# Two attentions of a two-block transformer kernel: a low part in eight pieces, a table loaded ahead, fewer fillers, key tiles one by one

## What is computed

```python
for i in range(DEPTH):                       # two layers
    hn = rms_norm(h, norm_pre[i])
    ...
    # layer 0: 12 heads, 64 + 32 rotary features; layer 1: 12 heads of 64, forget gates added to the logits
    main = mla_mixer(...) if i % 2 == 0 else fox_mixer(...)
    mem_out = memory_attention(q_m, k_m, v_m)      # 4 heads over 256 memory tokens
    y = jnp.concatenate([main, mem_out], axis=-1) * jax.nn.silu(gate)
    h = h + rms_norm(y @ w_out[i], norm_post[i])

def causal_block_attention(q, k, v, scale, log_f_cum=None):
    ...
    s = jnp.where(mask, s, -jnp.inf)
    p = jax.nn.softmax(s, axis=-1)
    return jnp.einsum('bhqk,bkhd->bqhd', p, v)
```

## Time and profile before

| | us |
|---|---|
| median of three runs | 1983.44 |
| lowest, highest | 1981.88, 1983.7 |
| the profiled execution's own time | 1981.69 |
| its span | 1980.0 |
| TensorE (PE) busy | 1931.6 (98%) |
| VectorE (DVE) busy | 1100.9 (56%) |
| GpSimd (POOL) busy | 786.6 (40%) |
| ScalarE (ACT) busy | 767.0 (39%) |

### The profile page before, as it was taken

One profiled execution on the slowest core, in us unless ns is written; L12 is line 12 of the kernel. 1 busy time (PEld: TensorE's weight loads), 2 busy tenths in 40 slices (PEclk: granted clock), 3 DMA queues, 4 the chain that ended last, 5 costly groups with the idle time before them and its releaser, 6 DMA issues.

```text
span 1980.0 us, 23818 instructions
## 1 busy us (share of the span) xinstructions
PE 1931.6 (98%) x9905; PEld 1538.7 (78%) x9905; DVE 1100.9 (56%) x1514; ACT 767.0 (39%) x1175; POOL 786.6 (40%) x345
## 2 busy tenths in 40 slices
PE   7999999999999999999999999999999999999998
PEld 6877566988657699977788888787977878888886
DVE  5333767557776659544678747865811355512533
ACT  5335554421463431265323223324376333222331
POOL 2233643433563452122343444343532434444432
PEclk9999999999999999999999999999999999999999
DMA  8224004365303351121254444453430222233221
GB/s 257 72 48 124 31 1 139 120 196 176 107 1 101 113 170 65 43 85 59 71 164 143 144 143 143 132 159 106 143 113 22 83 78 95 85 100 113 77 80 57
DMA packets 212059, 205.95 MB, mean 104 GB/s; under 512 B 21351, under 2 KB 209003, under 8 KB 211952
## 3 DMA queue, kind: packets, MB, share of 16 engines
q1 hardware_dynamic: 209369, 200.36, 31.6%
q0 software_dynamic: 1472, 3.72, 0.7%
q10 hardware_dynamic: 1111, 0.36, 0.1%
HBM read 201.44 MB, written 2.11 MB: 103 GB/s over the span
## 4 chain that ended last, share of the span: by engine, by line
PE 86%; ACT 4%; DVE 4%; POOL 2%; issue 1%; DMA 1%; ACTq 0%; SPq 0%; DVEq 0%
PE bank L543 55%; PE bank L1128 16%; PE bank L784 2%; PE bank L484 2%; POOL wl L2352 2%; PE bank L951 1%; PE bank L833 1%; PE bank L808 1%; DMA ring<-in_w_mem_kv 1%; PE bank L1186 1%; ACT probs L1488 1%; PE bank L1196 1%; ACT wh L1339 1%; PE bank L533 1%; PE bank L566 1%
## 5 line engine op out<-in xcount | busy, mean ns | idle before, releaser
L2352 POOL TENSOR_TENSOR wl<-ring,wh 128x2048 fp32r<-128x2048 f32 (+4 forms) x147 | 627.1, 4266 | 922.3 <-ACT wh L1339 920.7
L1339 ACT ACTIVATE wh<-ring 128x2048 fp32r<-128x2048 f32 (+4 forms) x147 | 256.4, 1744 | 304.0 <-PE bank L1128 130.1
L543 PE MATMUL bank<-xfh,wh 128*128 128x512 f32 x704 | 275.9, 392 | 0.0
L543 PE MATMUL bank<-xfh,wl 128*128 128x512 f32 x704 | 274.2, 390 | 0.0
L543 PE MATMUL bank<-xfl,wh 128*128 128x512 f32 x704 | 273.9, 389 | 0.0
L1783 DVE SCALAR_TENSOR_TENSOR acc<-ring,cs,acc 128x256 f32<-128x256 f32 x336 | 242.3, 721 | 12.0
L543 PEld LDWEIGHTS bank<-xfh,wh 128*128 128x128 f32 x704 | 132.2, 188 | 30.7 <-DVE xfl L1845 2.6
L543 PEld LDWEIGHTS bank<-xfh,wl 128*128 128x128 f32 x704 | 132.1, 188 | 27.8
L543 PEld LDWEIGHTS bank<-xfl,wh 128*128 128x128 f32 x704 | 132.2, 188 | 26.7
L2215 DVE SCALAR_TENSOR_TENSOR x<-bank,mod,x 128x512 f32<-128x512 f32 x48 | 34.8, 750 | 192.1 <-PE bank L1128 192.1
L1128 PE MATMUL bank<-hsph,wh 128*128 128x512 f32 x352 | 138.2, 393 | 2.1 <-POOL wl L2352 2.1
(11 more groups left out here) (407 smaller groups left out, 4164.8 us busy)
## 6 DMA issues: line engine op xcount, KB each, us to landing
ring<-in_ada_w SPq DMA_DIRECT2D x48, 1024.0 KB, 5.2
ring<-in_ffn_w_in SPq DMA_DIRECT2D x44, 1024.0 KB, 5.1
ring<-in_w_in_b SPq DMA_DIRECT2D x14, 1024.0 KB, 5.2
ring<-in_even_w_in SPq DMA_DIRECT2D x14, 1024.0 KB, 5.0
ring<-in_ffn_w_out SPq DMA_DIRECT2D x16, 768.0 KB, 4.3
ring<-in_odd_w_in SPq DMA_DIRECT2D x12, 1024.0 KB, 5.3
ring<-in_ffn_w_out SPq DMA_DIRECT2D x16, 640.0 KB, 4.6
ring<-in_w_out SPq DMA_DIRECT2D x8, 1024.0 KB, 5.2
```

The source lines that it names most:

```text
L543: mm = eng.matmul(o, l_, r_, start=(first and i == 0), stop=(last and i == 2))
L1339: eng.activation(wh[:, m % SPLIT, h:w], ring[:, n % RING, h:w], ACT.Copy).then_inc(wh_ready, 1)
L2352: eng.tensor_tensor(wl[:, m % SPLIT, h:w], ring[:, n % RING, h:w], wh[:, m % SPLIT, h:w].bitcast(F32), ALU.subtract).then_inc(wl_ready, 1)
```

## The change

- The second output chunk's low part is no longer made ahead of head 0, but in eight pieces of 256 columns, one behind GpSimd's part of each of the heads 0 to 7. `wl_ready` is counted with the last.
- Exp's table is loaded by a dummy activation: in layer 0 between the two halves of V tiles, in layer 1 ahead of the q and k chunks.
- The fillers go from six and nine to one each.
- The last two key tiles of layer 1 are made one after the other, not side by side.
- The wait for V's tiles moves from ahead of head 0's scores to the first `apply`.

```diff
@@ -39,6 +39,7 @@
 RING = 3
 SPLIT = 2
 CHUNK = 256
+PIECES = 8
 ROT = 6
 ADA_UNTIL = (18, 24, 36, 48)
 ACC = 2
@@ -815,6 +816,9 @@
                             wait_emptied(pe, ("o", l, pair - 1))
                         else:
                             pe.wait_ge(ssq_taken, counts["hn"])
+                            if l == 0:
+                                for c in range(2):
+                                    wait_emptied(pe, ("v", c, NB - 1))
                         for h in heads:
                             for g in range(3):
                                 wait_emptied(pe, ("t", l, h, g))
@@ -856,7 +860,7 @@
                     if h >= 3:
                         apply((h - 3) // 2, (h - 3) % 2)
                     if h == 1:
-                        warm((6, 9)[l], aside=True)
+                        warm(1, aside=True)
                     if h >= 1:
                         transposes(h - 1)
                 apply(6, 1)
@@ -880,8 +884,6 @@
             pe.wait_ge(const_ready, 4)
             pe.wait_ge(kf_ready, 16)
             pe.wait_ge(rope_done, HEADS)
-            for c in range(2):
-                wait_emptied(pe, ("v", c, NB - 1))
             attention(0)
 
             def out_first(l):
@@ -927,7 +929,12 @@
             project("in_b.qm", 1, "dve", "x_b", xb, lag=1)
             project("in_b.gate", 3, "dve", "x_b", xb, lag=1, t=2)
             project("in_b.q", 3, "dve", "x_b", xb, lag=1)
-            project("in_b.k", 3, "dve", "x_b", xb, lag=1)
+            project("in_b.k", 2, "dve", "x_b", xb, lag=1)
+            m, ws = chunk("in_b.k")
+            for t in range(2):
+                features(("in_b.k", 4 + t), "dve", ws, slice(t * P, (t + 1) * P), xb, KT, "x_b")
+            chunk_done(m)
+            ada_sums(1)
             mark["att1"] = len(released)
             for s in range(3):
                 wait_emptied(pe, ("in_b.v", s, NB - 1))
@@ -1391,6 +1398,10 @@
             def load_roots():
 
                 chain.link(eng.activation(early[:, :], ones[:, 0:1], ACT.Sqrt))
+
+            def load_exponentials():
+
+                chain.link(eng.activation(early[:, :], ones[:, 0:1], ACT.Exp))
 
             act.wait_ge(loaded_c, 16)
             load_roots()
@@ -1471,6 +1482,8 @@
             for c in range(2):
                 for blk in range(NB):
                     empty(("v", c, blk), v1[:, blk, 384 * c:384 * (c + 1)], part=(slice(0, P), slice(0, 384)))
+                if c == 0:
+                    load_exponentials()
 
             def attention(l):
                 split_weights(mark[f"att{l}"] + 2)
@@ -2364,14 +2378,28 @@
             eng.dma_start(kf[ropes, :, :], kr[ropes, :].unsqueeze(1).to_broadcast([ROPE, HEADS, S])
                           ).then_inc(kf_ready, 16)
 
+            def low_piece(m, i):
+
+                n = pe_at[m]
+                w = plan[n][2] * plan[n][3] // PIECES
+                cols = slice(i * w, (i + 1) * w)
+                pool.wait_ge(wh_ready, m + 1)
+                ins = eng.tensor_tensor(wl[:, m % SPLIT, cols], ring[:, n % RING, cols],
+                                        wh[:, m % SPLIT, cols].bitcast(F32), ALU.subtract)
+                if i == PIECES - 1:
+                    ins.then_inc(wl_ready, 1)
+                    low_done[0] += 1
+
             def attention(l):
-                low_weights(mark[f"att{l}"] + 2)
+                low_weights(mark[f"att{l}"] + 1)
                 for h in range(16):
                     par = h % 2
                     pool.wait_ge(rinv_ready, l * 16 + h + 1)
                     for i in range(NB - 1):
                         w = probs[:, par, packed(h, i):packed(h, i) + keys(h, i)]
                         eng.tensor_scalar(w, w, rinv[:, par, i:i + 1], None, ALU.mult).then_inc(probs_ready, 1)
+                    if h < PIECES:
+                        low_piece(mark[f"att{l}"] + 1, h)
 
             def residual(l):
 
```

## The result

| | before | after |
|---|---|---|
| median, us | 1982.74 (4 runs) | 1970.41 (4 runs) |
| lowest, highest | 1981.88, 1983.7 | 1969.34, 1972.17 |
| profiled execution, its span | 1981.69, 1980.0 | 1969.34, 1967.6 |
| TensorE busy | 1931.6 | 1916.9 |
| VectorE busy | 1100.9 | 1094.5 |

After against before: ratio 0.9938, interval 0.9925 to 0.995.

The account below looks back on a forecast made before the run. TensorE was taken to hold most of the chain, so only the two attention starts could be bought back: 5.9 + 3.4 - 0.4 = 8.9 us off the 1983.44 median gives 1974.5, range 1971.8 to 1979.5.

Parts of the forecast that it names:

- Edit 1: First attention's start: moving the second low part away and loading the table ahead brings inverse sums 5.9 us earlier.
- Edit 2: Second attention's start: the same move and early load, with key tiles emptied singly, gain 4.95 us before the load's cost.
- tile by tile: Second attention's last key tiles: emptying them one after the other gives only 0.28 us, limited by VectorE's modulation step.
- Its price: Table load ahead of the q and k chunks: delays ScalarE's split and low part, 1.53 us lost, leaving 3.4 gained.
- Edit 3: Heads 0 to 7 of both attentions: eight low-part pieces of 0.73 us each, costing 0.4 us in all.
- lead of 1.05: Settled heads: GpSimd's rows are ready about 1.05 us before TensorE wants them, so shorter delays cost nothing.
- Edit 4: Both attention starts: 5 and 8 fewer fillers give nothing by themselves; left in, the second's would run into earlier work.
- the sum: Whole kernel: gains of 5.9 and 3.4 us less a loss of 0.4 make 8.9 us.
- The pieces held nobody: Rival, both attentions: GpSimd's pieces hold VectorE, which holds TensorE; 1985.8 or 1990.9 us; chance 0.06.
- the load at 447: Rival, ahead of the second attention: the table load is hidden after all, 1.5 us stays, 1973.0 us; chance 0.09.
- The clock rival: Rival, attention starts: with few fillers the clock falls, 1.7 us each, 1976.2 to 1977.9 us; chance 0.14.
- A load that costs 1.38 more: Rival, load at 447 us: ScalarE must run empty first, 1.38 us more, 1975.9 us; chance 0.04.

## Why the prediction came out wrong

**Its mechanism held in the main.**

- Edit 1, gain 5.9: measured 6.08. The size is right, the reason only in part. The prediction let the scores come 0.5 earlier and had `nmx` freed by the idle GpSimd. `nmx` came 0.9 earlier, and with the whole low part left in place the inverse sums were as early (3.97). There the low part's move paid 6.5 us behind them, the clock included, a cost for which the prediction has no term. No run moves the low part and keeps V's wait, so what each would do alone is not shown. The load between the V tiles cost nothing: ScalarE again waits 0.55 for TensorE ahead of the last tile.
- Edit 2, gain 4.95: from the end of VectorE's modulation step to the inverse sums 11.04 became 6.04, 5.00. In it tile by tile was put at 0.28; the run with wide tiles leaves 0.1 to 0.3.
- Its price, 1.53: from the last gate to the first `wh` 2.62 became 4.12, and moving the load gave back 1.3. The second attention's 3.4 was 3.55 in the pair.
- Edit 3, pieces of 0.73 and loss 0.4: the pieces take 0.726, and their loss is nothing, since heads 1 to 12 run to the same time within 0.02. The lead of 1.05 in settled heads holds a piece and not a whole low part. The attentions are longer by 0.19 + 0.32 = 0.51 all the same, from head 13 on; that this is near 0.4 is luck.
- Edit 4, fillers: "removing them gives nothing by itself" was wrong by its sign. Alone it costs 5 us; what made it free is that the rest of the change shortens the wait they covered. Left in, the second attention's 18 passes take 7.94, as put; what that costs was not put. It is 5.1 us there and 2.5 in the first attention, which the prediction doesn't mention.

**What failed** is the last step, from the sum to the number: "I forecast against the median: 1983.44 - 8.9", with "runs differing by 1.8" as the allowance. The 1.8 was the distance between the lowest and the highest of three runs. The same program's 81 runs reach from 1977.71 to 1988.45, and 0.001 of mean granted clock goes with about 1.5 us in them. The prediction had a fall of the clock in its rows (0.72 from 40 to 46) and read it as what such a stretch does, where it was one execution's.

The miss of 4.1 us (1974.5 against 1970.41) has three parts. The 1983.44 lies 0.9 above the mean of before's 85 runs. The difference of the means is 10.5, 1.6 more than the sum; at an equal clock only 0.1 of that is left. And the median of the four runs of the result lies 1.7 below the mean of the changed kernel's 16. The sum was right to 0.2 us in the profiled pair, partly by luck (edit 3), and the range, reaching 2.7 below the forecast, was too narrow on its better side.

**The rivals.** The pieces held nobody, and the load at 447 was not hidden. The clock rival did not come true in the changed kernel, but it was the nearest to doing so: it did in three versions with one thing other than in the change (no loads, no filler, whole low part). Its price was off, too: 1.4 at the first start without the loads, but 3.8 to 4.6 at the second, where 1.7 was put. The stretch from 204 to 208 that the prediction reads as lying behind the fillers holds them until 206.78; its idle 1.2 us are the start of the wait of 1.44 shown above. A load that costs 1.38 more is refuted at this place: from the end of the last DMA issue to the first `wh` it took 1.56 (437.86 to 439.42), with the load and its activation in it. With the load behind the first split, the split ends at 439.52 and the load starts at 439.54. The Trainium skill, "ScalarE: Activation LUTs", "What ACT_TABLE_LOAD costs", has about 2.66 us for a switch, a drain among it; its 1283 ns are there, the drain is not to be seen here.

## What to carry to other kernels

A tiny instruction can be the longest of a start: look for one whose duration equals a neighbour engine's, and move the neighbour's work, cut into pieces shorter than the lead of the heads that take them in. Price filler matmuls together with the wait that they cover: too few lose the clock, too many stand in the way, and each change of the wait asks for a new count. Before holding a gain of half a per cent against a forecast, compare at an equal mean granted clock, or cut both spans into segments and count only those that the change touches.

## What the runs showed of the hardware

- Where TensorE waited 0.55 and 0.70, or 0.82 and 0.70, around three transposes, the clock stayed full. It stayed so with 1.44 and 0.70 (before) and 1.46 and 0.70 (no filler), and fell to 1.2 GHz in the profiles with 1.73 and 0.70 (no filler, second start), 1.96 and 0.70, 2.01 and 0.54 (no early loads), 2.64 and 0.70, 4.59 and 0.64 (whole low part), and 5.73 and 0.34 (one filler, else as before). Each is a single profile. Elsewhere (100 to 108, 332 to 344) the clock fell in one execution of a program and not in another.
- A VectorE instruction of 0.35 us is stretched to the end of GpSimd's operation in other places than `nmx`. Two rows of the changed kernel, GpSimd first, and one of the same form 13 us later, between two of GpSimd's low parts:

```profile
446.14 4.64 POOL L2366 TENSOR_TENSOR wl<-ring,wh 128x2048 fp32r<-128x2048 f32 x1
```

```profile
446.31 4.62 DVE L1795 TENSOR_SCALAR acc<-ring,cs 128x256 f32<-128x256 f32 x1
...
459.43 0.35 DVE L1795 TENSOR_SCALAR acc<-ring,cs 128x256 f32<-128x256 f32 x1
```

Not every VectorE instruction is held: in the run with the whole low part ahead of head 0, a row maximum of 128x512 out of a bank takes 0.69 at 201.48, in the midst of the low part, and 0.69 in the changed kernel, where none runs. The Trainium skill, "SBUF — State Buffer", "SBUF: two separate sides", tells of the lock by which one of the two waits for the other's whole instruction, for certain VectorE instructions; the traces agree in the places where one was held (4.62 here, 3.96, 2.59 and 3.05 above).
